# Expert layer: gather in f32r halves, second half inside experts 0 and 1, return selection built per pair

## The reference

```python
def ec_moe(h, router, w1, w3, w2):                     # h: 512 tokens x 1024
    cap = EC_CAPACITY * n // N_EXPERTS                 # 2 * 512 // 16 = 64
    aff = softmax(h @ router)                          # 512 x 16
    gate, idx = lax.top_k(aff.T, cap)                  # each expert picks its 64 tokens
    xe = h[idx]                                        # 16 x 64 x 1024
    hid = silu(xe @ w1) * (xe @ w3)                    # per expert, width 1024
    ye = (hid @ w2) * gate[..., None]
    return zeros_like(h).at[idx].add(ye)
```

## Time and profile before

| | |
|---|---|
| median of 3 runs | 5205.73 us (5204.96 to 5208.75) |
| span of the profiled execution | 5216.1 us, 10.4 us above that median |
| own time of the profiled execution | not recorded beside the span; the span stands for it |
| mean granted TensorE clock | 0.927 |
| `moe` in the trace, from its first load to its last instruction | 2360.6 to 2962.7 us |

### The profile page before, as it was taken

The page is one execution under the profiler, slowest core; times in us unless marked ns, Lnnn a source line. Parts: engine busy times, 40 slices in busy tenths (PEclk is TensorE's granted clock), DMA queues, the critical chain, the costliest instruction groups (busy, mean ns, idle before and its releaser), DMA issues. The chain is left out here.

```text
span 5216.1 us, 87974 instructions
## 1 busy us (share of the span) xinstructions
PE 4445.1 (85%) x38358; PEld 3430.0 (66%) x38358; DVE 2553.7 (49%) x3625; ACT 1587.3 (30%) x2492; POOL 544.8 (10%) x496
## 2 busy tenths in 40 slices
PE   7999968888887678786888786789999899687999
PEld 5888857777776456563222264467888787576787
DVE  4556666667775665542111224654443312575553
ACT  3222223333332453431000124433222211563332
POOL 0000021111110356000000002310000000000000
PEclk9999979999998789897999998889999999898999
DMA  6656710000000020422999731021122133112232
GB/s 243 228 192 216 273 59 22 15 14 14 14 6 31 25 69 17 167 84 99 420 421 421 291 103 36 18 100 53 61 65 71 62 112 123 67 60 79 85 100 94
DMA packets 165534, 604.11 MB, mean 116 GB/s; under 512 B 24032, under 2 KB 37216, under 8 KB 139808
## 3 DMA queue, kind: packets, MB, share of 16 engines
q1 hardware_dynamic: 151920, 538.72, 28.8%
q0 software_dynamic: 13232, 59.77, 2.9%
HBM read 526.97 MB, written 71.46 MB: 115 GB/s over the span
## 5 line engine op out<-in xcount | busy, mean ns | idle before, releaser
L1903 PE MATMUL f_acc<-f_a_lo,f_w_hi 128*128 128x512 f32 x4048 | 1037.0, 359 | 63.0 <-DVE f_a_lo L2125 29.0
L1903 PEld LDWEIGHTS f_acc<-f_a_lo,f_w_hi 128*128 128x128 f32 x4048 | 668.9, 190 | 189.0 <-issue 42.6
L1903 PE MATMUL f_acc<-f_a_lo,f_w_lo 128*128 128x512 f32 x2288 | 691.9, 358 | 0.0
L1892 DVE TENSOR_TENSOR f_w_lo<-f_w_raw,f_w_hi 128x1024 fp32r<-128x1024 f32 (+1 forms) x176 | 228.3, 1298 | 542.9 <-ACT f_w_hi L1887 542.9
L1903 PEld LDWEIGHTS f_acc<-f_a_lo,f_w_lo 128*128 128x128 f32 x2288 | 380.8, 190 | 66.2
L1887 ACT CAST f_w_hi<-f_w_raw 128x1024 fp32r<-128x1024 f32 (+1 forms) x176 | 194.7, 1106 | 613.8 <-DMA f_w_raw<-in_ffn_w_up 221.0
L1903 PE MATMUL i_acc<-i_x_hi,i_w_hi 128*128 128x512 f32 (+1 forms) x1024 | 308.4, 357 | 13.5 <-DVE i_x_lo L2680 10.0
L352 DVE COPY_PREDICATED rw_work<-rw_mask_x,rw_big 128x512 f32<-128x512 uint8 x288 | 238.7, 881 | 155.4 <-PE rw_big L642 150.2
L1903 PE MATMUL i_acc<-i_x_hi,i_w_lo 128*128 128x512 f32 (+1 forms) x1024 | 310.7, 359 | 0.0
L1903 PE MATMUL i_acc<-i_x_lo,i_w_hi 128*128 128x512 f32 (+1 forms) x1024 | 307.2, 356 | 0.0
L642 PE MATMUL rw_big<-rw_work,rw_halves 128*64 128x64 f32 x4608 | 260.8, 222 | 2.0 <-issue 1.9
(11 more groups left out here) (518 smaller groups left out, 8083.6 us busy)
## 6 DMA issues: line engine op xcount, KB each, us to landing
ex_w<-in_exp_w SPq DMA_DIRECT2D x192, 1024.0 KB, 16.6
i_mod_rows<-in_ada_rows SPq DMA_DIRECT2D x128, 512.0 KB, 4.7
f_w_raw<-in_ffn_w_up SPq DMA_DIRECT2D x88, 512.0 KB, 3.5
i_w_raw<-in_w_in_both SPq DMA_DIRECT2D x44, 512.0 KB, 3.6
f_w_raw<-in_ffn_w_down SPq DMA_DIRECT2D x32, 704.0 KB, 4.1
i_w_raw<-in_w_in_lat SPq DMA_DIRECT2D x40, 512.0 KB, 4.5
pt<-i_stage POOLq DMA_DIRECT2D x22, 768.0 KB, 6.0
f_w_raw<-in_hgrn_w_both SPq DMA_DIRECT2D x24, 512.0 KB, 3.6
```

Of the source, the lines that this page charges most:

```text
L1892: dve.tensor_tensor(self.view(self.w_lo, u), self.view(self.w_raw, u), self.view(self.w_hi, u).bitcast(F32), ALU.subtract).then_inc(self.r ...
L1903: op = pe.matmul(acc[:, a:b], part[:, k], xs[:, k0 + k, a:b], start=(first and k == 0 and part is w_hi and xs is x_hi), stop=(last and k = ...
```

## The change

- Tokens are split into a rounded part `htok_hi` (ScalarE) and a remainder `htok_lo` (VectorE), both float32r. A gather group is then 8 float32r matmuls (4 token tiles x 2 parts) in place of 4 float32 ones.
- The one-hot is built per half (eight experts each). The first half is gathered ahead of the experts (groups 0 to 7); of the second, four groups stand inside expert 0 and four inside expert 1, after the up product.
- The transposes of `ht` stand ahead of the logits, over six banks of PSUM in place of two.
- `weighted`, its transposes and the copies into `sel` are gone. In place of them each pair of experts has, in its odd expert, two float32 matmuls of a 16-row selector `pick` with the slot rows and the affinity rows (`choose`), and two VectorE operations (`chosen`).
- `onehot` now lies in the memory of `ht`, `sel` in that of `htok_lo`. The first loads of w2 wait for nothing.
- The products read `xe` itself; `xe_now` and its copies on GpSimd are gone.
- `ht` has a semaphore of its own; there are two more small loads, `slot_of` (128 x 1) and `pick` (16 x 1024).

```diff
+        ht_at = -(-nc.sbuf_base // 32) * 32
+        ht = sb("ht", [P, KD, LAT])
+        lo_at = ht_at + KD * LAT * 4
+        htok_lo, htok_hi = sb("htok_lo", [P, 4, D], F32R), sb("htok_hi", [P, 4, D], F32R)
+        onehot, sel = over("onehot", [P, 2, 4, 512], F32R, ht_at), over("sel", [P, PAIRS, LAT], F32, lo_at)
-        xe_now = [sb(f"xe_now{s}", [P, KD, CAP]) for s in range(2)]
-        onehot, weighted = (w2s[s][:]... for s in range(2))
+        def gather_bank(n):
+            return 4 + n % 2 if n < KD else back_bank((n - KD) // 4, n)
 # sync
+                sp.dma_start(ht[:], h_in[:, 0:LAT]...).then_inc(S["ht_in"], 16)
+                for dst, src in ((slots[:], consts["slots"]), (slot_of[:], consts["slot_of"]), (pick[:], consts["pick"])):
+                    sp.dma_start(dst, src).then_inc(S["loaded"], 16)
-                        elif kh == 0:
-                            sp.wait_ge(S["sel_copied"], 8)
 # tensor
-                pe.wait_ge(S["loaded"], 64)
+                pe.wait_ge(S["loaded"], 80)
+                pe.wait_ge(S["ht_in"], 16)
+                for n in range(8):
+                    t, half = n // 2, n % 2
+                    if n >= 6:
+                        pe.wait_ge(S["ht_split"], n - 5)
+                    for q in range(4):
+                        last = pe.transpose(big[:, 2 + n % 6, q * P:(q + 1) * P], ht[:, 4 * half + q, t * P:(t + 1) * P], ident[:])
+                    last.then_inc(S["ht_ready"], 1)
                 for t in range(4):
                     for k in range(KD):
                         last = pe.matmul(big[:, 0, t * 16:t * 16 + 16], ht[...], wr[:, k], ...)
...
+                def gather(n):
+                    half, k = n // KD, n % KD
+                    if k == 0:
+                        pe.wait_ge(S["hot_done"], half + 1)
                     if n >= 2:
                         pe.wait_ge(S["xe_copied"], n - 1)
                     for t in range(4):
-                        last = pe.matmul(big[:, 4 + n % 2, :], htok[:, t, k * P:(k + 1) * P], onehot[:, t, half * 512:half * 512 + 512], ...)
+                        for part in (htok_hi, htok_lo):
+                            last = pe.matmul(big[:, gather_bank(n), :], part[:, t, k * P:(k + 1) * P], onehot[:, half, t], ...)
                     last.then_inc(S["xe_ready"], 1)
+                def choose(e, pair):
+                    pe.matmul(big[:, back_bank(e, 0), :], pick[:, pair], work[:, 2], start=True, stop=True)
+                    pe.matmul(big[:, back_bank(e, 1), :], pick[:, pair], work[:, 3], start=True, stop=True).then_inc(S["sel_ready"], 1)
+                for n in range(KD):
+                    gather(n)
                 for e in range(N_EXP):
-                    pe.wait_ge(xe_ready, e + 1)
+                    if e == 0:
+                        pe.wait_ge(S["xe_copied"], KD)
+                    if e == KD:
+                        pe.wait_ge(S["xe_copied"], 2 * KD)
...
+                        pe.wait_ge(S["sel_done"], pair)
                         bring_back(e, pair - 1, range(4 * par, 4 * par + 4))
                         pe.wait_ge(back_done, KD * (pair - 1) + 4 * par + 4)
+                    else:
+                        for n in range(KD + 4 * e, KD + 4 * e + 4):
+                            gather(n)
+                        pe.wait_ge(S["xe_copied"], KD + 4 * e + 4)
+                    if par:
+                        choose(e, pair)
                     pe.wait_ge(hid_done, e + 1)
+                    if par:
+                        pe.wait_ge(S["sel_done"], pair + 1)
 # vector
+                    dve.tensor_tensor(htok_lo[part], big[:, 2 + n % 6, :], htok_hi[part].bitcast(F32), ALU.subtract).then_inc(S["ht_split"], 1)
...
+                def chosen(e, pair):
+                    dve.wait_ge(S["sel_ready"], pair + 1)
+                    dve.tensor_scalar(sel[:, pair], big[:, back_bank(e, 0), :], slot_of[:, 0:1], None, ALU.is_equal)
+                    dve.drain()
+                    dve.tensor_tensor(sel[:, pair], sel[:, pair], big[:, back_bank(e, 1), :], ALU.mult).then_inc(S["sel_done"], 1)
```

More of the change, by code:

```diff
@@ L1220, in moe @@
         slot_t = sb("slot_t", [P, 4, N_EXP])
[L1221 to L1222 removed]
+        xe = sb("xe", [P, KD, N_EXP * CAP])
         w13 = [sb(f"w13_{s}", [P, 2, 2, KH, 512]) for s in range(2)]
         w2s = [sb(f"w2_{s}", [P, 2, KH, 512]) for s in range(2)]
[L1225 removed]
         sg, hid = sb("sg", [P, 512]), sb("hid", [P, 512])
@@ L1275, in _ @@
                 last.then_inc(S["logits"], 1)
[L1277 to L1283, removed]
                 pe.wait_ge(S["aff_done"], 1)
@@ L1291, in _ @@
                 last.then_inc(S["cols_ready"], 1)
[L1292 to L1295, removed]
+                pe.wait_ge(S["ht_split"], 8)
+                def gather(n):
+                    half, k = n // KD, n % KD
+                    if k == 0:
+                        pe.wait_ge(S["hot_done"], half + 1)
                     if n >= 2:
@@ L1298, in _ @@
                     for t in range(4):
-                        last = pe.matmul(big[:, 4 + n % 2, :], htok[:, t, k * P:(k + 1) * P], onehot[:, t, half * 512:half * 512 + 512], start=(t == 0), stop=(t == 3))
+                        for part in (htok_hi, htok_lo):
+                            last = pe.matmul(big[:, gather_bank(n), :], part[:, t, k * P:(k + 1) * P], onehot[:, half, t], start=(t == 0 and part is htok_hi), stop=(t == 3 and part is htok_lo))
                     last.then_inc(S["xe_ready"], 1)
[L1301 to L1307, removed]
+                def choose(e, pair):
+                    pe.matmul(big[:, back_bank(e, 0), :], pick[:, pair], work[:, 2], start=True, stop=True)
+                    pe.matmul(big[:, back_bank(e, 1), :], pick[:, pair], work[:, 3], start=True, stop=True).then_inc(S["sel_ready"], 1)
                 def bring_back(e, pair, ds):
@@ L1323, in _ @@
                                 for half in range(2):
-                                    last = pe.matmul(big[64 * half:64 * half + 64, 2 * par + m, :], xe_now[par][:, kh * KH + k],
+                                    last = pe.matmul(big[64 * half:64 * half + 64, 2 * par + m, :], xe[:, kh * KH + k, e * CAP:(e + 1) * CAP],
                                                      w13[kh][:, m, half, k], start=(kh == 0 and k == 0), stop=(kh == 1 and k == KH - 1))
@@ L1365, in _ @@
                     act.activation(sg[:], big[:, 2 * par, :], ACT.Sigmoid).then_inc(act_done, 1)
+                    if pair == 0:
+                        for n in range(KD + 4 * e, KD + 4 * e + 4):
+                            gathered(n)
                     act.wait_ge(down_ready, 2 * e + 2)
@@ L1374, in _ @@
                 dve.memset(ones[:], 1.0)
+                for n in range(8):
+                    dve.wait_ge(S["ht_copied"], n + 1)
+                    part = (slice(None), n // 2, slice((n % 2) * 512, (n % 2) * 512 + 512))
+                    dve.tensor_tensor(htok_lo[part], big[:, 2 + n % 6, :], htok_hi[part].bitcast(F32), ALU.subtract).then_inc(S["ht_split"], 1)
                 dve.wait_ge(S["logits"], 1)
@@ L1406, in _ @@
                 dve.drain()
[L1407 to L1417, removed]
+                for half in range(2):
+                    for t in range(4):
+                        last = dve.tensor_tensor(onehot[:, half, t].rearrange("p (e c) -> p e c", c=CAP), slot_t[:, t, 8 * half:8 * half + 8].unsqueeze(2).to_broadcast([P, 8, CAP]),
+                                                 slots[:].unsqueeze(1).to_broadcast([P, 8, CAP]), ALU.is_equal)
+                    last.then_inc(S["hot_done"], 1)
+                def chosen(e, pair):
[3 more added lines that the diff above has]
+                    dve.tensor_tensor(sel[:, pair], sel[:, pair], big[:, back_bank(e, 1), :], ALU.mult).then_inc(S["sel_done"], 1)
                 def add_back(e, pair, ds):
@@ L1438, in _ @@
                         add_back(e, pair - 1, range(4 * par, 4 * par + 4))
+                    if par:
+                        chosen(e, pair)
                     dve.wait_ge(turned_ready, e + 1)
```

54 lines of the change are left out of this document (27 added, 27 removed).

## The result

The changed kernel takes 5175.85 us (median of 4 runs, 5174.20 to 5176.29) against 5205.34 us before; the ratio is 0.9945, 95% interval 0.9931 to 0.9960, so 21 to 36 us are gained. Forecast were 5161 us and a range of 5151 to 5172: the direction is right, a third of the gain is missing, and the time lies outside the range.

What follows compares the result with a forecast made beforehand. The prediction took the expert layer to be held by its router wait, then its weight stream. Stream end 47.3 us earlier plus 2.65 us of `choose` in the tail gave -44.6, so 5205.7 became 5161 us; range 5151 to 5172.

Steps and rivals of the forecast that it cites:

- What bounds the kernel before: Expert layer: load 8 MiB, stand still until the router is done, stream 184 MiB without holes, then a TensorE tail.
- The start of the router: Router: small loads cost 0 (-0.5 to +0.5 us); transposes ahead of logits 0, between 4.4 us earlier and 3.3 later.
- rival A: Router: the clock stays up through the logits, 4.4 us earlier, 5157 us, down to 5151 with fewer holes; chance 0.14.
- One-hot and gather: Ahead of the experts: first half of the gather takes 16.7 us, expert 0 starts at 2427.8 instead of 2475.31.
- The second stream: Expert weights: 180 MiB, data from 2436.5, holes of 4.0 us (0 to 8), ending 47.3 us earlier.
- `choose`: Odd experts: two matmuls, two VectorE operations and signals hold TensorE 2.65 us (1.0 to 4), once more in the tail.
- TensorE keeps up by 2.5 us: Experts: a pair costs TensorE 58.7 us against 59.8 of stream, so the stream still decides, by 2.5 us.
- Both signs of being wrong: Experts: TensorE never waits for weights and the stream has holes after expert 3; together they would refute the forecast.
- B: Experts: TensorE becomes the bound; seven slow up halves add 12 us, leaving 10 on the end, 5171 us; chance 0.13.
- C: First experts: holes eat the early w2's gain, 4 MiB or 10 us less, 5171 us; chance 0.06.
- D: Experts: TensorE without rest gets a mean clock of 0.88 or less, slower than before; chance 0.03.
- E: Whole layer: no change, because the layer isn't held by its start; chance 0.02.

Runs made afterwards that it cites:

- choose_early: Changed kernel with `choose` and `chosen` moved ahead of the odd expert's up product from pair 1 on; 5156.95 us.
- late_w2: Changed kernel in which the first load of w2 waits again, for the eighth copy of the gather; 5172.52 us.
- pair0_late_w2: pair0_late in which the first load of w2 waits again for the eighth copy of the gather; 5153.06 us.
- no_choose_matmuls: Changed kernel without the two matmuls of `choose` from pair 1 on, VectorE's operations and the wait for `sel` kept; 5164.91 us.
- choose_no_wait: Changed kernel with `choose` in place but in banks 4 and 6, and `sel` waited for one expert later; 5159.65 us.
- gather_f32: Changed kernel with the gather in float32, one part and tokens not rounded, all else kept; 5200.36 us.
- pair0_late: choose_early with pair 0's `choose` also moved, from inside expert 1 to ahead of expert 2; 5151.57 us.

## Why the prediction was wrong

- **What bounds the kernel before**: right. All that was read from the earlier trace rows held.
- **The start of the router**: the five small loads beside `ht` cost 0.9 us (10.7 from the first load to TensorE's start, 9.8 before) where I had 0.5 at most; the last of them, `pick`, released TensorE. The order of transposes and logits gave 0 in this profile, and 3 us in others (rival A's mechanism, for part of the logits). The 0 of the sum was the middle between two ends and no mechanism, so that it came out in this profile is luck.
- **One-hot and gather**: right, 16.3 us against 16.7 for the first gather. That expert 0 starts at 67.4 us against 67.2 needs the luck above too: with the short router it starts at 64.2, as in choose_early.
- **The second stream**: its start was right (2436.75 - 2362.20 = 74.6 us into the layer, forecast 74.2). Its holes behind the first experts were larger than the 4.0 us of the sum, about 7 (estimate: 388 GB/s over the 91.6 us from 2438.4 to 2530, against 421). The 10 us of 4 MiB less stand in the sum beside a start 7.0 us later, behind the first half of expert 0's up product, and beside the 4.0 of holes, so its own terms gave the early w2 nothing (10.0 - 7.0 - 4.0); late_w2 and pair0_late_w2 measure nothing.
- **`choose`**: this is the step that failed. The sum gave it and what it does to its expert 2.65 us, with 4 as the upper bound; an odd expert came out 5.77 us longer than an even one. Of the missing 3.12 us, 1.02 are the price of the matmuls and of the wait for them. I took 0.43 us for a float32 matmul of 512 columns, from a row that counts records, and such a matmul is two records: the 118 in 50 us in the earlier trace rows are records, or 59 matmuls. So `choose` and its wait were 3.67 us and not 2.65. The same slip made no error in the gather, because the forecast took float32r's own count from the earlier trace rows and a float32r matmul is one record (64 in the first half). The counts in the kernel's description and in the prediction are records too: the logits are 32 matmuls in the source, half an up product 16, half a down product 8.
- **Not in the sum at all**: the clock, 2.10 us per odd expert, for the work behind `choose`. I had costed the wait by what is queued behind it, and not by the clock at which that then runs. This could have been read in the trace of before. There TensorE waits 2.19 us for `hid` in experts 0 and 1, where nothing is brought back, and the down products behind take 8.65 and 8.46 us and not 7.09. Expert 0, and the stretch around it:

```profile
2491.46 0.66 PE L1334 MATMUL ex_big<-ex_ident,ex_hid 128*128 128x128 f32 x4 [2.19 <-DVE ex_hid L1436]
2492.89 8.65 PE L1343 MATMUL ex_big<-ex_w,ex_hid_t 128*64 128x512 f32 x32 [0.78 <-DVE ex_hid_t L1442]
```
```profile
2490.00:2500.00 10.00, 7.76 (x30) 2.69 (x32) 2.01 (x3) 0.00 (x0) 0.00 (x0) 0.83 1.01 418
```

- **TensorE keeps up by 2.5 us**: so it did not. Both signs of being wrong that the prediction named together came: TensorE never waited for weights, and the stream had holes after expert 3 (408 to 414 GB/s in each 100 us between 2500 and 2900, against 421). To the second up half of expert 15 there are seven odd experts: 7 x (5.77 - 2.65) = 21.8 us more, and 15 x 0.22 = 3.3 less, for experts took 27.81 and not 28.03. That takes the 2.5 us and 16.0 more. Expert 15 itself adds another 3.1 and loses 1.7, because its up half took 6.9 us and not 8.7. Measured, the layer is 579.0 - 561.4 = 17.6 us longer than forecast; 16.0 + 1.4 of it are accounted for so. The other check is choose_early: with the changed kernel's router it takes 560.9 us, and the forecast was 561.4.
- **The rivals**: B had the right bound and nearly the time (5171), but it priced it by slow up halves behind waits for weights; what came were slow down products behind `choose`. C's sign, 10 us of holes more than the 4, did not come (about 7 in all), but its reason, that the holes eat what the early w2 saves, is what pair0_late_w2 shows. D's slower clock came, 0.93 to 0.97 per 100 us between 2500 and 2900, but far from its 0.88. E fell.

## What to carry to other kernels

When an edit adds a wait or a matmul of few rows to an engine that has a few per cent of slack, add what the clock takes from the dense work behind it (look in the trace for a place where the engine already pauses so), and ask whether the same work can stand between two dense products: here that one choice was worth 18 us, two thirds of the whole change again. Before a matmul's price is taken from a count, check with the source how many records one instruction makes. And moving bytes ahead of a wait gains only what the stream can't fill in another way.

## What the runs showed of the hardware

- The granted clock fell to 0.50 within the experts after 2.29 us of idleness (no_choose_matmuls, odd experts from 3 on) or after 1.9 us of 16-row matmuls (choose_no_wait, the same experts), each with waits of 0.8 to 0.9 us on both sides. The 16-row matmuls between dense products left it at 1.00 (choose_early, 2521.00 to 2526.00).
- A wait of about 2 us between the two halves of an up product came out both ways. In the kernel before, the half behind a wait of 1.46 to 1.81 us took 7.09 us, and behind waits of 2.00, 2.16, 2.75 and 3.02 us it took 8.6 to 8.8. But behind waits of 2.04 and 2.22 us in choose_early it took 7.09. What else decides was not tried.
- A float32 matmul of 512 columns costs nearly twice what its two float32r parts cost together: the first half of the gather took 29.7 us in gather_f32 (32 matmuls, 64 records) and 16.3 in the changed kernel (64 matmuls, 64 records).
- The logits, 64 records of 16 columns, ran at 0.50 before. With 32 transposes ahead of them the clock rose and then fell again while TensorE was busy throughout (columns as in the earlier trace rows):

```profile
2377.00:2379.00 2.00, 2.00 (x15) 2.00 (x14) 1.52 (x4) 1.46 (x4) 0.00 (x0) 0.67 1.00 418
2379.00:2381.00 2.00, 2.00 (x21) 2.00 (x20) 1.83 (x3) 0.92 (x2) 0.00 (x0) 1.00 1.03 430
2381.00:2383.00 2.00, 2.00 (x15) 2.00 (x14) 0.00 (x0) 0.00 (x0) 0.00 (x0) 0.69 0.99 414
2383.00:2385.00 2.00, 2.00 (x11) 2.00 (x11) 0.00 (x0) 0.00 (x0) 0.00 (x0) 0.50 1.03 430
```

  In choose_early and pair0_late the logits took 9.4 and 9.3 us and the transposes 5.0 and 5.2; here it was 11.2 and 6.3. That is the 3 us by which the router's length varies. Before, the logits took 13.8. What decides between the two lengths was not tried.
- The Trainium skill (TensorE: Matmul & The Clock Gate, Part 1: The HAM clock gate) says that sustained matmul activity brings the high clock and idleness the low one. The rows of the experts agree on idleness, but for the two waits in choose_early above. On activity they go only part of the way with it: the clock rose over the 32 transposes above, but fell from 1.00 to 0.50 between 2381 and 2385 while TensorE was busy throughout with the 16-column records, and in before it stayed at 0.50 through 13.7 us of them.
